# Letting the weight queue run on past the end of each layer's experts in a four-layer diffusion backbone

## What is computed

```
x = x + mod[:, None, 2] * y                       # y: the mixer's output
h = modulate(rmsnorm(x, norm_ffn[i]), mod[:, 3], mod[:, 4])
...
hid = jax.nn.silu(jnp.einsum("td,edf->tef", x, wg)) * jnp.einsum("td,edf->tef", x, wu)
hid = hid * combine[..., None]                    # weights of the two chosen experts, 0 elsewhere
y = jnp.einsum("tef,efd->td", hid, wd)
x = x + mod[:, None, 5] * y
```

## Time and profile before

| what | value |
|---|---|
| runs of the kernel | 1293.26 and 1298.45 us, median 1295.86 |
| the profiled execution | 1297.72 us |
| its span, first to last instruction | 1295.9 us |
| what lies around the span | 1.8 us |
| PE busy | 1170.8 us, 90% of the span |
| DVE, ACT, POOL busy | 45%, 25%, 10% |
| mean traffic | 301 GB/s, 389.56 MB |
| q1, the weights | 336.61 MB, 66.1% of the DMA engines' time |
| q0, POOL's DMAs | 51.07 MB, 10.9% |
| the chain that ended last | PE 73%, DMA 11%, DVE 4% |

### The profile page before, as it was taken

One profiled execution on the slowest core, in us unless ns is written; L12 is line 12 of the kernel. 1 busy time (PEld: TensorE's weight loads), 2 busy tenths in 40 slices (PEclk: granted clock), 3 DMA queues, 4 the chain that ended last, 5 costly groups with the idle time before them and its releaser, 6 DMA issues.

```text
span 1295.9 us, 24580 instructions
## 1 busy us (share of the span) xinstructions
PE 1170.8 (90%) x10198; PEld 710.0 (55%) x10198; DVE 582.6 (45%) x1347; ACT 330.4 (25%) x724; POOL 123.3 (10%) x188
## 2 busy tenths in 40 slices
PE   4788998889999889799987999999799997799986
PEld 2346554346886545565545844555565545575544
DVE  1355211259651639731117876459741115741113
ACT  1240111241112640411115411340411114411113
POOL 2000110201000000011120000000011120011101
PEclk9898998989999999899999999899899998799998
DMA  9999999798774577398989973107489987578983
GB/s 354 406 422 419 417 406 421 292 386 321 263 283 161 207 268 307 132 373 345 387 325 356 395 281 129 53 1 276 163 326 356 411 336 296 225 297 339 385 369 138
DMA packets 89708, 389.56 MB, mean 301 GB/s; under 512 B 10456, under 2 KB 38604, under 8 KB 53240
## 3 DMA queue, kind: packets, MB, share of 16 engines
q1 hardware_dynamic: 71568, 336.61, 66.1%
q0 software_dynamic: 17456, 51.07, 10.9%
q10 hardware_dynamic: 568, 0.23, 0.1%
HBM read 370.96 MB, written 27.96 MB: 308 GB/s over the span
## 4 chain that ended last, share of the span: by engine, by line
PE 73%; DMA 11%; DVE 4%; ACT 3%; SPq 3%; issue 3%; POOL 1%; POOLq 0%; DVEq 0%; ACTq 0%
PE bank L531 67%; DMA sb_ring<-in_w_ada 3%; PE bank L1081 3%; SPq L489 3%; DMA sb_ring<-in_w_exp_down 2%; DMA slot_out<-sb_arena,sb_homes 2%; DMA sb_arena<-slot_out,sb_slots 2%; DMA token_rows<-sb_arena 1%; POOL sb_arena L2354 1%; PE bank L1099 1%; DVE sb_xT L2207 1%; DVE sb_hT L1687 1%; PE bank L1030 1%; DMA sb_arena<-token_rows,sb_rows 1%; ACT sb_hT L1353 1%
## 5 line engine op out<-in xcount | busy, mean ns | idle before, releaser
L531 PE MATMUL bank<-sb_ring,sb_arena 128*32 128x256 f32 (+1 forms) x6112 | 456.8, 430 | 19.4 <-DMA sb_ring<-in_w_exp_down 6.0
L531 PEld LDWEIGHTS bank<-sb_ring,sb_arena 128*32 128x32 f32 x6112 | 227.1, 112 | 190.9 <-issue 113.0
L531 PE MATMUL bank<-sb_arena 128*128 128x128 f32 (+11 forms) x776 | 137.0, 354 | 9.0 <-ACT sb_arena L1513 2.3
L531 PE MATMUL bank<-sb_ring,sb_hT 128*128 128x256 f32 x624 | 141.3, 388 | 4.2 <-ACT sb_hT L1343 4.2
L1677 DVE SCALAR_TENSOR_TENSOR sb_arena<-sb_ring,sb_cond,sb_arena 128x2048 f32<-128x2048 f32 (+1 forms) x70 | 139.1, 2024 | 11.9 <-ACT sb_scratch L1313 11.7
L531 PEld LDWEIGHTS bank<-sb_ring,sb_hT 128*128 128x128 f32 x624 | 120.2, 194 | 25.8 <-issue 8.7
L2154 DVE TENSOR_TENSOR sb_arena<-sb_arena,bank 128x256 f32<-128x256 f32 x40 | 16.8, 421 | 259.0 <-PE bank L531 259.0
L531 PEld LDWEIGHTS bank<-sb_arena 128*128 128x128 f32 (+2 forms) x776 | 99.2, 188 | 43.5 <-issue 21.7
L531 PE MATMUL bank<-sb_arena,sb_ring 128*128 128x384 f32 (+2 forms) x288 | 93.9, 501 | 0.0
L531 PE MATMUL bank<-sb_hT,sb_ring 128*128 128x384 f32 x256 | 86.3, 500 | 2.6 <-ACT sb_hT L1343 2.6
L2161 DVE COPY sb_arena<-bank 128x512 f32<-128x512 f32 x40 | 27.7, 692 | 130.9 <-PE bank L531 130.9
(11 more groups left out here) (343 smaller groups left out, 1168.2 us busy)
## 6 DMA issues: line engine op xcount, KB each, us to landing
sb_ring<-in_w_ada SPq DMA_DIRECT2D x96, 1024.0 KB
sb_ring<-in_w_exp_gate SPq DMA_DIRECT2D x60, 1024.0 KB
sb_ring<-in_w_exp_up SPq DMA_DIRECT2D x60, 1024.0 KB
sb_ring<-in_w_exp_down SPq DMA_DIRECT2D x60, 1024.0 KB
sb_ring<-in_w_mlstm_in SPq DMA_DIRECT2D x12, 1024.0 KB
token_rows<-sb_arena POOLq DMA_DIRECT2D x12, 512.0 KB, 3.9
slot_out<-sb_arena POOLq DMA_DIRECT2D x9, 512.0 KB, 9.1
sb_scratch<-in_w_exp_gate SPq DMA_DIRECT2D x4, 1024.0 KB
```

What stands on the lines that cost most here:

```text
L531: return pe.matmul(out, lhsT, rhs, start=first, stop=last)
```

## The change

The dictionary and both places that use it are removed. The units, their order and the waits for a slot's release stay. Lines behind the removed ones move up by up to 7 (L489 becomes L482).

```
-        hold = {}
         ada_units(0)
         for L in range(LAYERS):
...
-            hold[len(units) + 3 * (NE - 1)] = (yg_in[NT - 1], 32 * (L + 1))
-            if L == LAYERS - 2:
-                hold[len(units) + 3 * (NE - 1) + 1] = (ms_full, 2 * (2 * L + 2) + 1)
-
...
                 if u >= RING:
                     done, value = units[u - RING][2]
                     sp.wait_ge(done, value)
-                if u in hold:
-                    sp.wait_ge(*hold[u])
```

## The result

| kernel | runs | median | profiled execution, span |
|---|---|---|---|
| before | 1293.26 and 1298.45 us | 1295.86 us | 1297.72, 1295.9 us |
| after | 1323.18 and 1331.22 us | 1327.2 us | 1323.18, 1321.3 us |

The ratio of after to before is 1.0245 [1.02, 1.0291]. The forecast was 1324.0 with a range of 1308 to 1340. PE is busy for 1171.1 us (1170.8 before), so the change added no work. It made PE wait. The interval begins at 2%, so this measurement alone does not settle whether the loss is over 2%.

What follows compares the result with a forecast made beforehand. Bound: the last store and six gathers at three layer ends. 6.1 + 4.8 + 15.1 + 1 (clock) = 27.0 us on the profiled 1297.7 gave 1324.7; that execution lying 1.9 us above the median, 1324 was given, range 1308 to 1340.

Steps and rivals of the forecast that it cites:

- What bounds a layer end: At three layer ends, last store then six gathers are on the path; whatever lengthens a gather lengthens the program one for one.
- Turns packet by packet: In the DMA engines, q0 and q1 alternate single packets; q0 gets 142 GB/s beside 8 KB rows, 270 beside 1 KB.
- rival B: Worse: q0 has 142 GB/s at the first two layer ends as well; 44.5 us, about 1342; chance 0.18.
- Layer 2: Third set of gathers, all beside expert matrices: 26.8 instead of 12.5 us; +15.1 us with the store.
- Layer 0: First set of gathers, beside mixed m and a units: 18.3 instead of 12.7 us; +6.1 us with the store.
- Layer 1: Second set of gathers, beside the second m unit: 4 + 11.5 + 1 = 16.5 instead of 12.4 us; +4.8 with the store.
- The stores: Last stores of expert results at the three layer ends, with q1 full to the end: 0.5, 0.7 and 0.8 us more.
- The clock: PE idles 26 us more before short chains of matmuls, so its granted clock is lower: +1 us (0 to 4).
- Early weights at nothing: Weights of layers 1 to 3 arrive 15 to 25 us earlier but nobody waits for them: 0 (0 to -3).
- A: Milder cost at the layer ends: half the extra start delay, +2.5, +3 and +11, about 1314; chance 0.27.
- C: Not slower: DMA engines serve q0 first, gathers keep 12.5 us, early weights save up to 3 us; 1295 to 1298; chance 0.04.
- D: Slots are released so late that q1 is dry at the layer ends anyway; 1297; chance 0.01.

Runs made afterwards that it cites:

- the second run: The changed kernel, no holds at any layer end, measured again in more rounds against the kernel before: ratio 1.0283 [1.0239, 1.0327].
- only layer 0 free: The kernel before with the hold missing only at layer 0's end; the other layer ends keep theirs: ratio 1.0073.
- only layer 2 free: The kernel before with both holds missing at layer 2's end only; the other layer ends keep theirs: ratio 1.0135.
- the single ends: Three kernels, each the kernel before without its hold at one layer end (layers 0, 1, 2 in turn): ratios 1.0073, 1.0058 and 1.0135.
- `w_pool` alone: The kernel before without layer 2's first hold, so only that unit goes out at once; expert matrices stay held: ratio 1.0003 [0.9972, 1.0034].
- the shorter hold: The kernel before, each first hold released by the first pair of gathers instead of the last: ratio 1.0051 [1.0026, 1.0076].
- the kernel with 2 KB rows at layer 2: The changed kernel with layer 3's first 11 expert units loaded in rows of 2 KB instead of 8 KB: ratio 1.0167 to the kernel before, 1317.0 us.

## Why the prediction was right, and where its numbers were off

- **What bounds a layer end: right.** The gathers are on the path at every end: what a set lost in a run, its time lost. SP's 115 us of waiting cost nobody anything, and taking them away won nothing.
- **Turns packet by packet: right.** It was read from 9 us and 3 us of layer 0 and doubted for indirect loads. 769 to 774 packets beside 8 KB rows, 638 to 667 beside mostly 1 KB rows, and 901 to 933 beside 2 KB rows show it for gathers too. The Trainium skill ("DMA: Bandwidth & Descriptors", Queues, rings and completion order) says that an engine drains some 9 to 17 descriptors of one queue before it turns to the next. Such counts do not decide that, since equal runs on both sides give one to one as well; for the same reason it does not follow from the page that the sum would come out near rival B's. The start and length of the single records in the trace decide it, and the trace does not agree with the page: of the data records in 1080 to 1096 us of the changed kernel, 521 of q0 and 555 of q1, 926 begin 3 or 4 ns before one of the other queue ends, where chance gives about 72, and 221 begin 2 or 3 ns after one of their own queue ends, where chance gives about 73. So the engines changed the queue after most single records.
- **Layer 2: 26.8 us forecast, 28.1 measured** (27.4 in the second run). The rate was 132 GB/s where I took 142, from the earlier trace rows, which is 1.7 us more. The start was 4.2 us where I took 4, and the last packet took less than the 1 us that I gave it (0.6 us at layers 0 and 1, from the end of the last gather record to the landing). The terms were also not laid out alike: a set alone would be 1.3 + 11.5 + 1 = 13.8 us by them, where 12.5 was measured and subtracted, so each end was forecast about 1 us too dear by this alone, which hid part of the errors in the transfers.
- **Layer 0: 18.3 forecast, 19.4 measured.** The mixed sequence of m and a units came out as it was laid out: 178 records to 181 in 249 to 253 us beside mostly 8 KB rows, then 311 to 306 in 253 to 257 us beside mostly 1 KB rows.
- **Layer 1: 16.5 forecast, 21.0 measured.** This is the mis-sized term, the 11.5 us of transfer in 4 + 11.5 + 1. The start came as forecast: q0's first record begins at 681.6 us, 4.2 us after the first issue. The step said that the gathers meet only the second m unit, which lasts 14 us at 73 GB/s. That held for most of them: 90% of the gather records had begun by 691.7 us. But 8 KB rows were back before the gathers were through, and the last 0.25 MB took the 6 us from 692 on. The transfer as a whole, from the first record to the end of the last, took 16.2 us. The step had taken the second m unit as lasting equally long on all engines; that they were out of step is my reading, and no run shows it engine by engine. With the a units in 2 KB rows too the set took 16.2 us in all, so the tail did come from the size of the rows.
- **The stores: +2.0 forecast, nothing measured.** They sum to 24.4 us in the chain (24.8 in the second run), 24.7 before. That q1 ran dry under them in the kernel before did not shorten them.
- **The clock: +1 forecast, none to be told from the noise.** PE idles longer at layer 2, and its granted clock is at the lower level, 1.2 GHz, when the last gather lands. The changed kernel by windows (busy us of PE, PEld, DVE, ACT and POOL, then PEclk, DMA share, GB/s):

```profile
1090.00:1100.00 10.00, 0.48 (x1) 0.18 (x1) 1.29 (x1) 1.15 (x1) 0.00 (x0) 0.50 1.02 420
1100.00:1110.00 10.00, 7.65 (x39) 5.39 (x40) 6.62 (x18) 6.58 (x9) 0.00 (x0) 0.69 0.73 303
1110.00:1120.00 10.00, 7.55 (x49) 5.83 (x48) 6.63 (x20) 6.79 (x18) 0.00 (x0) 0.66 0.01 2
```

  PE does one matmul in 10 us there, at 0.50, and has 0.69 and 0.66 in the 20 us in which the norm begins, where the kernel before had 0.84 in 1070 to 1080 us and 0.99 in 1080 to 1090 us. The mean granted clock of the span was 0.947 in the changed kernel's profile and 0.956 before. A cost of it does not show: from the landing of the third set to the first fetch of layer 3's token rows the kernel before took 65.3 us and the changed kernel 66.7 and 66.6 us, but the kernel with only layer 0 free, whose third set is short, also took 66.7 us, and the one with only layer 2 free, whose set is as long as in the changed kernel, 63.7 us. Nor do the 6 us between "more" and "time" of the second run stand in its profiled execution, whose span is 30.4 us above that of the kernel before with sets 30.7 us longer. No run isolates the clock, and those 6 us stay open.
- **Early weights at nothing: right.** The sum over the single ends, and `w_pool` alone, leave no gain. What I had not said is how little room there is on the other side: 9 us later costs about 7.
- **The total: in the range, and nearer than its terms by luck.** The forecast of 27.0 had 24.0 for the sets (5.6, 4.1 and 14.3), 2.0 for the stores and 1 for the clock. The sets cost 30.9, so that term was 6.9 too low, mostly at layer 1. On the profiled execution 25.5 us were lost (1323.18 less 1297.72), because the stretches between the sets came out 5.5 us shorter in all, 5.1 of them in the one stretch that differs by 12 us from profile to profile. That is luck, and it hid the error. Between the medians the loss was 31.3 us, and 36.7 us when it was measured again; the forecast of 1324 lies 3.2 us under the median of 1327.2.
- **Rivals.** A (the cost is milder) and C (q0 goes first) fall with the third set: 28.1 us, where A had about 23.5 and C 12.5. B had layers 0 and 1 as slow as layer 2, 27 us; they took 19 and 21. D falls with SP's waits.

## What to carry to other kernels

An idle weight queue is not a loss where nothing waits for what it holds back; look for the one who waits before filling it. When a short, urgent transfer is on the path, keep bulk transfers out of the DMA engines until its last byte has landed, and release them then, not later: here a release at the first of three pairs cost 6.6 us and one 9 us late cost 7.5 us. Where they can't be kept out, split them into small rows, since the share of a queue was set by the size of its neighbour's packets; but not where the weights themselves are what is waited for.

## What was not expected of the hardware

- The last of a set is dearer than its share. At layer 1, 82 of its 864 packets took the last 6 us while q1 made 464, so q0 was getting far less than every second turn over all 16 engines. I read it as a few engines that still had gather packets while the others had none; no run tests that by itself.
- The bytes in all did not suffer. During the third set the engines moved 8.31 MB in 20 us (5.66 and 2.65), 416 GB/s, more than the 270 of the gathers alone (3.24 MB in 12 us with their start). The change moved more bytes in that stretch and was slower for it.
- Gathers that have all been issued, and whose only neighbour is a single 1 MB unit of 1 KB rows, still pay some 2 us: with the shorter hold the last gather of layer 2 was issued at 1077.06 us and `w_pool` at 1077.51 us, and the set took 14.4 us.
- The late start was as long beside 2 KB rows as beside 8 KB rows. The prediction took 4 us for the latter; beside 2 KB rows q0 also had no record in the first 4.2 us (1075.1 to 1079.3 us of the kernel with 2 KB rows at layer 2). Beside 1 KB rows, at layer 0, the first record came after 2.1 us, but the first 5% of them took until 4.3 us, where the kernel before needed 2.7 us. What the 4 us consist of, no run shows.
